# Four instruction orders of an attention stage rearranged: projections later, one evacuation on VectorE, weight splits earlier

## The chip, the cores and the metric

The kernel runs on one core of a Trainium2 chip. A core has a matrix engine (TensorE, PE in the profile, with its weight loads as PEld), a vector engine (VectorE, DVE), a scalar engine (ScalarE, ACT), GpSimd (POOL) and a queue that issues DMAs (SyncE, SP). Each engine works its own instruction list strictly in order and waits at semaphores for the others. The metric is the device time of one execution in microseconds (us), lower is better. The median of three runs before the change is 2721.38 us (2718.41 to 2723.39).

## The reference

Two layers of an encoder trunk are computed for 512 prompt tokens and for 8 running streams of 16 tokens (640 tokens in 5 tiles of 128). Each layer is a half SwiGLU, a mixer, another half SwiGLU and a gated embedding, with layer norms between. The mixer of the second layer is stick-breaking attention over 16 heads of 64; the streams also attend to 1024 cached keys each. What the change touches is this:

```python
def sb_core(q, k, v, q_pos, k_pos):
    z = jnp.einsum('bqhd,bkhd->bhqk', q, k) * SB_SCALE
    mask = k_pos[None, :] < q_pos[:, None]
    log_keep = jnp.where(mask, jax.nn.log_sigmoid(-z), 0.0)
    after = lax.cumsum(log_keep, axis=3, reverse=True) - log_keep
    w = jnp.where(mask, jnp.exp(jax.nn.log_sigmoid(z) + after), 0.0)
    return jnp.einsum('bhqk,bkhd->bqhd', w.astype(v.dtype), v)
```

## The kernel before

The program is a list of stages (`plan_stages`), each written out by hand for every engine. Weights arrive by DMA in units of 512 KB into three slots of `raw`; ACT copies a unit's high part into `ring` (line 970), DVE subtracts to get the low part (line 1285), and every product is made of three matmuls (line 1645). This pair of instructions is called a weight split here.

The attention stage takes the heads as eight pairs, i = 0 to 7. Each pair has ten units of scores (`UNITS`), numbered 0 to 9: units 2, 5, 8 and 9 are the cached samples, the others the prompt. Unit g = 10 i + u passes through a fixed chain:

- PE `scores` writes z to one of four PSUM banks (line 499 helper);
- DVE `neg_abs` (line 1390) writes -|z|, and for samples also max(z, 0) (line 1396);
- ACT `exp_ln` takes Exp and Ln (lines 1032, 1034);
- DVE `softplus` (line 1406) for prompt units, or `sample_sums` (a scan, line 1429, and a subtraction, line 1432) for samples; for samples ACT then does `sample_rows` (Exp, line 1040);
- PE `suffix` (two sums by triangular matrices for prompt units, four transposes at line 605 for samples);
- ACT `weights` (line 1049), PE `values` with the value rows.

Beside the units run the "events" (`STEP_EVENTS`): results that PE writes to just two PSUM banks, 6 and 7, in turn. They are the projections qA, qB, kA, kB of the next pair (A is 384 columns, B is 256), the transposed cached keys kT (su, j) of sample su, each with four transposes (line 531), the transposed own keys kt4 and kt1 (line 522), the totals `tot`, and `past` (line 549), the sample outputs of the pair before. Before PE may write event number k it waits until event k - 2 has been evacuated (`event_bank`). Even kT events, kt4 and all projections are evacuated by ACT (lines 1016, 1018, 1023), odd kT events, kt1, tot and past by DVE (lines 1360, 1362, 1364, 1371). After qB has been evacuated, DVE copies its sample columns into `q_blk` (`sample_queries`, line 1380).

SP issues the cached keys (`load_keys`, line 761) and values (`load_values`, line 771), four DMAs of 256 KB for each sample, and weight units (line 739). Values of a sample wait for `values` of the sample two before, and everything behind them in the queue waits too. In the last pair (i = 7) there is no projection; in its place ACT and DVE split the attention output (`split_o`, lines 1055 and 1438) and the first units of the output weights, and PE begins the output product (`out_early`) as soon as it can.

## Time and profile before

| | us |
|---|---|
| median of three runs | 2721.38 |
| lowest, highest | 2718.41, 2723.39 |
| the profiled execution's own time | 2718.41 |
| its span in the profile | 2716.4 |
| attention stage, first scores of pair 0 to first scores of pair 7 | 1673.74 to 2031.87 |
| first matmul of the output product | 2079.45 |

| engine | busy us | share of the span |
|---|---|---|
| PE | 2591.2 | 95% |
| PEld | 2313.9 | 85% |
| DVE | 1105.0 | 41% |
| ACT | 851.5 | 31% |
| POOL | 78.0 | 3% |

Times in the trace are microseconds from the span's start. A row of a timeline gives the start and the length of a group of like instructions, and in brackets how long the engine sat idle before it and what ended the idleness. Two starts on one engine give the pitch, which is shorter than the lengths printed, since instructions overlap a little in their ends.

### The profile page before, as it was taken

The numbers are of one execution on the slowest core, as the hardware profiler recorded it, in microseconds if no ns is written. First come the engines' busy times: TensorE is split into PE (matmuls) and PEld (weight loads), VectorE is DVE, ScalarE is ACT, GpSimd is POOL, SyncE is SP. The second block draws the span as 40 slices with busy tenths as digits, with TensorE's granted clock in tenths as the row PEclk, the third lists the DMA queues.
The fourth block names the chain that finished last, engine by engine and source line by source line (L and its number), as shares of the span: only waits on it lengthen the run. The fifth ranks groups of instructions, "written<-read, shape, count | busy, mean of one in ns | idle before, by whom it ended". The sixth has DMA issues, their size and how long they took to land. (4 is left out here: it accounts for less than half of the span.)

```text
span 2716.4 us, 37476 instructions
## 1 busy us (share of the span) xinstructions
PE 2591.2 (95%) x16164; PEld 2313.9 (85%) x16164; DVE 1105.0 (41%) x1521; ACT 851.5 (31%) x1271; POOL 78.0 (3%) x169
## 2 busy tenths in 40 slices
PE   7999999989999998899999999999998999999987
PEld 7998998789989987799899877666665899899876
DVE  3322334553232245633233342555555632232365
ACT  3212222232122223522122233555555322132133
POOL 3000000100000000000000001000000000000000
PEclk9999999889999998999999999999999999999999
DMA  5213221322132212232132215666765322232220
GB/s 163 78 59 90 78 69 56 95 80 69 58 94 74 74 59 86 77 92 68 54 105 71 72 60 153 183 177 188 207 181 167 92 86 74 59 94 78 65 90 39
DMA packets 376612, 259.07 MB, mean 95 GB/s; under 512 B 10433, under 2 KB 339137, under 8 KB 376448
## 3 DMA queue, kind: packets, MB, share of 16 engines
q1 hardware_dynamic: 371344, 239.64, 30.3%
q0 software_dynamic: 5104, 17.04, 2.0%
q8 instruction: 128, 2.10, 0.3%
q14 instruction: 36, 0.29, 0.0%
HBM read 248.22 MB, written 8.42 MB: 94 GB/s over the span
## 5 line engine op out<-in xcount | busy, mean ns | idle before, releaser
L1645 PE MATMUL ps<-xt_hi,ring 128*128 128x384 f32 (+1 forms) x6144 | 1353.1, 311 | 37.2 <-DVE xt_lo L1345 15.7
L1645 PEld LDWEIGHTS ps<-xt_hi,ring 128*128 128x128 f32 x6144 | 1042.6, 191 | 53.2 <-issue 20.9
L1645 PE MATMUL ps<-xt_lo,ring 128*128 128x256 f32 (+1 forms) x3072 | 952.5, 310 | 0.0
L1645 PEld LDWEIGHTS ps<-xt_lo,ring 128*128 128x128 f32 x3072 | 586.6, 191 | 0.2
L1645 PE MATMUL ps<-ring,h_hi 128*128 128x512 f32 x1760 | 549.9, 392 | 0.0
L970 ACT ACTIVATE ring<-raw 128x1024 fp32r<-128x1024 f32 x326 | 324.8, 1028 | 442.7 <-PE ps L1645 351.1
L1285 DVE TENSOR_TENSOR ring<-raw,ring 128x1024 fp32r<-128x1024 f32 x326 | 381.7, 1198 | 160.7 <-ACT ring L970 156.5
L1645 PEld LDWEIGHTS ps<-ring,h_hi 128*128 128x128 f32 x1760 | 332.6, 189 | 69.0
L1528 DVE SCALAR_TENSOR_TENSOR act<-act,ps 128x384 f32<-128x384 f32 (+1 forms) x176 | 85.9, 488 | 689.1 <-PE ps L1645 689.1
L1645 PE MATMUL ps<-ring,h_lo 128*128 128x512 f32 x880 | 344.2, 391 | 0.0
L1183 ACT ACTIVATE h_hi<-act 128x384 fp32r<-128x384 f32 (+1 forms) x176 | 82.8, 471 | 647.7 <-DVE act L1528 647.7
L1645 PE MATMUL ps<-ring,xt_hi 128*128 128x512 f32 (+1 forms) x720 | 230.3, 394 | 19.5 <-DVE ring L1285 15.6
L1645 PEld LDWEIGHTS ps<-ring,h_lo 128*128 128x128 f32 x880 | 166.4, 189 | 34.0
L1645 PEld LDWEIGHTS ps<-ring,xt_hi 128*128 128x128 f32 x720 | 139.4, 198 | 50.1 <-DVE ring L1285 14.4
L1177 ACT ACTIVATE act<-ps 128x384 f32<-128x384 f32 (+1 forms) x176 | 77.0, 437 | 255.3 <-PE ps L1645 253.4
L1645 PE MATMUL ps<-ring,xt_lo 128*128 128x512 f32 (+1 forms) x360 | 140.4, 390 | 0.0
L1534 DVE TENSOR_TENSOR h_lo<-act,h_hi 128x384 fp32r<-128x384 f32 (+1 forms) x176 | 86.5, 492 | 92.2 <-ACT h_hi L1183 92.2
L1320 DVE SCALAR_TENSOR_TENSOR x<-x,ps 128x512 f32<-128x512 f32 x50 | 34.2, 685 | 185.6 <-PE ps L1645 185.6
L1645 PEld LDWEIGHTS ps<-ring,xt_lo 128*128 128x128 f32 x360 | 71.4, 198 | 12.5
L531 PEld LDWEIGHTS ps<-ident,k_raw 128*128 128x128 f32 x512 | 56.1, 141 | 30.2 <-issue 19.4
L531 PE MATMUL ps<-ident,k_raw 128*128 128x128 f32 x512 | 70.8, 277 | 10.9 <-DMA k_raw<-in_cache_k_dram 6.8
L1390 DVE TENSOR_SCALAR e_buf<-ps 128x512 int32<-128x512 int32 (+1 forms) x80 | 51.5, 661 | 65.7 <-PE ps L499 65.5
(128 smaller groups left out, 1527.1 us busy)
## 6 DMA issues: line engine op xcount, KB each, us to landing
raw<-in_ffn_w_dram SPq DMA_DIRECT2D x256, 512.0 KB, 4.3
k_raw<-in_cache_k_dram SPq DMA_DIRECT2D x128, 256.0 KB, 5.2
v_raw<-in_cache_v_dram SPq DMA_DIRECT2D x128, 256.0 KB, 4.1
raw<-in_sb_w_in_dram SPq DMA_DIRECT2D x24, 512.0 KB, 6.2
raw<-in_ple_w_gate_dram SPq DMA_DIRECT2D x16, 512.0 KB, 4.1
g_b<-in_ln_g_dram POOLq DMA_DIRECT2D x8, 512.0 KB, 4.1
b_b<-in_ln_b_dram POOLq DMA_DIRECT2D x8, 512.0 KB, 5.5
raw<-in_ffn_w_dram SPq DMA_DIRECT2D x16, 256.0 KB, 3.5
```

Of the source, the lines that this page charges most:

```text
L531: ins = pe.transpose(ps[:, bank, kb * P:(kb + 1) * P], k_raw[:, sample % 2, j, kb, :], ident[:])
L970: se.activation(ring[:, slot_of(u), 0, 0:cols_in(u)], raw[:, raw_slot(u), 0:cols_in(u)], ACT.Copy).then_inc(w_hi_done, 1)
L1177: se.activation(act[:, PART[p]], ps[:, 2 * ((n - 1) % 2), 0:PART[p].stop - PART[p].start], ACT.Silu).then_inc(act_done, 1)
L1183: se.activation(h_hi[:, i, PART[p]], act[:, PART[p]], ACT.Copy).then_inc(h_hi_done, 1)
L1285: ve.tensor_tensor(ring[:, slot_of(u), 1, 0:n], raw[:, raw_slot(u), 0:n], ring[:, slot_of(u), 0, 0:n].bitcast(F32), ALU.subtract).then_inc ...
L1320: ve.scalar_tensor_tensor(dst, dst, ALPHA, ps[:, n % 4, :], ALU.mult, ALU.add).then_inc(x_upd, 1)
L1390: ve.tensor_scalar(e_buf[:, g % 2, 0:n].bitcast(I32), ps[:, g % 4, 0:n].bitcast(I32), SIGN, None, ALU.bitwise_or).then_inc(na_done, 1)
L1528: ve.scalar_tensor_tensor(act[:, PART[p]], act[:, PART[p]], 0.5, ps[:, 2 * ((n - 1) % 2) + 1, 0:PART[p].stop - PART[p].start], ALU.mult, A ...
L1534: ve.tensor_tensor(h_lo[:, i, PART[p]], act[:, PART[p]], h_hi[:, i, PART[p]].bitcast(F32), ALU.subtract).then_inc(h_lo_done, 1)
L1645: return pe.matmul(out, w, xx, start=first, stop=last, skip_group_check=True)
```

## The change

Only orders change, and one evacuation changes engines. No instruction is dropped; on DVE the evacuation of qB is new, on ACT it is gone.

- PE: `suffix` of unit 9 of the pair before moves ahead of projection qA; qB moves behind `suffix` 2 and `values` 1; `past` moves from before `scores` 5 to behind the transposes of kT (2, 0) and (2, 1); kA moves behind `suffix` 5 and `values` 4.
- ACT: `sample_rows` 9 goes behind `exp_ln` 0, `sample_rows` 2 ahead of kT (1, 2), `sample_rows` 5 behind `exp_ln` 6, and `sample_rows` 8 behind `weights` 7 and `exp_ln` 9. The evacuation of kT (0, 0) of the next pair goes behind these two. The weight split of unit 2i + 4 moves from after `exp_ln` 7 to before `exp_ln` 6, and so on DVE from after `softplus` 7 to before `neg_abs` 6.
- DVE: evacuates qB and builds `q_blk` at the end of step 4; `past` goes behind kT (2, 1).
- Last pair: the split of the first three output units moves ahead of unit 8 on both engines. SP loads them one and a half samples later.

```diff
-    4: [("qB",), ("past",)],
-    5: [("kT", 2, 0), ("kT", 2, 1)],
+    4: [("qB",)],
+    5: [("kT", 2, 0), ("kT", 2, 1), ("past",)],
-ON_ACT = ("qA", "qB", "kA", "kB", "kt4")
+ON_ACT = ("qA", "kA", "kB", "kt4")
...
                     values(i - 1, 7)
+                    suffix(i - 1, 9)
                 if follows:
                     project(i + 1, ("qA",))
-                if i:
-                    suffix(i - 1, 9)
...
+                suffix(i, 2)
+                values(i, 1)
                 if follows:
                     project(i + 1, ("qB",))
-                suffix(i, 2)
-                values(i, 1)
-                if i:
-                    transpose_past(i - 1, ("past",))
 
                 scores(i, 5)
                 suffix(i, 3)
                 turn_keys(i, 2, 0)
+                if i:
+                    transpose_past(i - 1, ("past",))
...
+                suffix(i, 5)
+                values(i, 4)
                 if follows:
                     project(i + 1, ("kA",))
-                suffix(i, 5)
-                values(i, 4)
...
-                if i == PAIRS - 2 and su == 2:
+                if i == PAIRS - 1 and su == 0:
                     for key in load_order[raw_at[first_out]:raw_at[first_out] + RAWS]:
...
                     exp_ln(g + 3)
+                    sample_rows(i, 2)
                     turned(i, 1, 1)
...
                     turned(i, 2, 0)
+                    if i < PAIRS - 2:
+                        cvt_to(first_qk + 2 * i + 5)
...
+                    exp_ln(g + 6)
                     sample_rows(i, 5)
-                    exp_ln(g + 6)
...
+                elif name == "qB":
+                    cols = PART[1]
+                    ve.tensor_scalar(q_t[i % 2][:, cols], src[:, 0:cols.stop - cols.start], SCALE, None,
+                                     ALU.mult).then_inc(aux_free_dve, 1)
+                    if i == 0:
+                        ve.wait_ge(q_blk_zero, 2)
+                    ve.wait_ge(aux_free_dve, count)
+                    for h in range(2):
+                        rows = slice(HEAD_DIM * h, HEAD_DIM * (h + 1))
+                        ve.tensor_copy(q_blk[i % 2][rows, :, h, :],
+                                       q_t[i % 2][rows, SEQ:].rearrange("p (b s) -> p b s", s=DEC_SEQ)
+                                       ).then_inc(q_blk_done, 1)
```

On DVE, in pair 4, the rows from `softplus` 3 and 4 (`sp_p`) to `neg_abs` 6 and 7 (`e_buf`, x2) stood like this before (`v_tok` is past, `ring` would be the weight split, line numbers are each kernel's own):

```order
L1406 SCALAR_TENSOR_TENSOR sp_p<-ps,e_buf 128x384 x2
L1371 TENSOR_TENSOR v_tok<-v_tok,ps 64x128 x2
L1390 TENSOR_SCALAR e_buf<-ps 128x512
L1396 TENSOR_SCALAR relu_s<-ps 128x512
L1360 COPY kc_t<-ps 128x512
L1429 SCALAR_TENSOR_TENSOR s_sum<-e_buf,s_sum,relu_s 128x512
L1432 TENSOR_TENSOR relu_s<-ps,s_sum 128x512
L1380 COPY q_blk<-act 64x8x16 x2
L1390 TENSOR_SCALAR e_buf<-ps 128x512 x2
```

The same stretch of the changed kernel:

```order
L1410 SCALAR_TENSOR_TENSOR sp_p<-ps,e_buf 128x384 x2
L1369 TENSOR_SCALAR act<-ps 128x256
L1376 COPY q_blk<-act 64x8x16 x2
L1394 TENSOR_SCALAR e_buf<-ps 128x512
L1400 TENSOR_SCALAR relu_s<-ps 128x512
L1362 COPY kc_t<-ps 128x512
L1385 TENSOR_TENSOR v_tok<-v_tok,ps 64x128 x2
L1433 SCALAR_TENSOR_TENSOR s_sum<-e_buf,s_sum,relu_s 128x512
L1436 TENSOR_TENSOR relu_s<-ps,s_sum 128x512
L1287 TENSOR_TENSOR ring<-raw,ring 128x1024
L1394 TENSOR_SCALAR e_buf<-ps 128x512 x2
```

The evacuation of qB and `q_blk` stand ahead of `neg_abs` 5 now, past stands ahead of the scan of unit 5, and the weight split ahead of `neg_abs` 6 and 7.

On ACT, at the end of pair 3, from kT (3, 2) of this pair to kt4 of the next (`k_tok`), the rows before (`relu_s` is `sample_rows` 8, `wt` is `weights` 7, the second `kc_t` is kT (0, 0) of the next pair, `e_buf` is `exp_ln` 9):

```order
L1016 ACTIVATE kc_t<-ps 128x512
L1040 ACTIVATE relu_s<-relu_s 128x512
L1049 ACTIVATE wt<-ps 128x512
L1016 ACTIVATE kc_t<-ps 128x512
L1032 ACTIVATE e_buf<-e_buf 128x512
L1034 ACTIVATE e_buf<-e_buf 128x512
L1018 ACTIVATE k_tok<-ps 128x512
```

The same stretch of the changed kernel:

```order
L1015 ACTIVATE kc_t<-ps 128x512
L1048 ACTIVATE wt<-ps 128x512
L1031 ACTIVATE e_buf<-e_buf 128x512
L1033 ACTIVATE e_buf<-e_buf 128x512
L1039 ACTIVATE relu_s<-relu_s 128x512
L1015 ACTIVATE kc_t<-ps 128x512
L1017 ACTIVATE k_tok<-ps 128x512
```

The evacuation of kT (0, 0) stood ahead of the Exp and Ln of unit 9 and stands behind them and `sample_rows` 8 now; PE's transposes of kt4 write the bank that it frees.

On ACT in the last pair, from `exp_ln` 7 to `exp_ln` 8 and kT (3, 0), the rows before (`xt_hi` is `split_o`, `ring` the split of output weights):

```order
L1032 ACTIVATE e_buf<-e_buf 128x512
L1034 ACTIVATE e_buf<-e_buf 128x512
L1055 ACTIVATE xt_hi<-v_tok 128x640 x4
L1049 ACTIVATE wt<-ps 128x512
L1032 ACTIVATE e_buf<-e_buf 128x512
L1034 ACTIVATE e_buf<-e_buf 128x512
L1016 ACTIVATE kc_t<-ps 128x512
```

The same stretch of the changed kernel:

```order
L1031 ACTIVATE e_buf<-e_buf 128x512
L1033 ACTIVATE e_buf<-e_buf 128x512
L1048 ACTIVATE wt<-ps 128x512
L1054 ACTIVATE xt_hi<-v_tok 128x640 x2
L969 ACTIVATE ring<-raw 128x1024 x3
L1031 ACTIVATE e_buf<-e_buf 128x512
L1033 ACTIVATE e_buf<-e_buf 128x512
L1015 ACTIVATE kc_t<-ps 128x512
```

The three splits of output weights (`ring`, x3) stand ahead of `exp_ln` 8 now, and on DVE ahead of `neg_abs` 8. Before, they stood behind `exp_ln` 9, four in a row.

## Rows read from the trace of the kernel before

**Rows 1.** The page's first part: busy time of each engine, share, instructions.

```profile
PE 2591.2 (95%) x16164; PEld 2313.9 (85%) x16164; DVE 1105.0 (41%) x1521; ACT 851.5 (31%) x1271; POOL 78.0 (3%) x169
```

**Rows 2.** Busy time by stretch: pair 3, and the output product's start.

```profile
core 0: us, PE busy (x) PEld busy (x) DVE busy (x) ACT busy (x) POOL busy (x), PEclk, DMA share, GB/s
1825.92:1877.60 51.68, 48.90 (x430) 34.79 (x430) 29.41 (x47) 28.64 (x52) 3.69 (x6) 1.00 0.69 190
2079.40:2084.30 4.90, 4.85 (x12) 3.82 (x13) 2.17 (x2) 0.92 (x1) 0.00 (x0) 0.50 0.73 197
```

**Rows 3.** Timeline of PE through pair 3: start, length, instruction, idle before.

```profile
1825.92 1.15 PE L499 MATMUL ps<-act,k_t 64*128 64x128 f32 x12
...
1830.46 0.41 PE L1645 MATMUL ps<-xt_hi,ring 128*128 128x384 f32 x1 [0.34 <-ACT kc_t L1016]
...
1843.94 0.39 PE L1645 MATMUL ps<-xt_hi,ring 128*128 128x256 f32 x1
...
1847.45 1.09 PE L499 MATMUL ps<-wt,v_tok 128*64 128x128 f32 x12
1848.47 0.44 PE L549 MATMUL ps<-ident,o_past 128*128 128x128 f32 x2
...
1851.93 1.09 PE L531 MATMUL ps<-ident,k_raw 128*128 128x128 f32 x8 [0.76 <-DMA k_raw<-in_cache_k_dram]
1852.95 1.13 PE L499 MATMUL ps<-act,k_t 64*128 64x512 f32 x4
...
1858.86 0.41 PE L1645 MATMUL ps<-xt_hi,ring 128*128 128x384 f32 x1 [1.42 <-ACT kc_t L1016]
...
1864.42 1.06 PE L499 MATMUL ps<-kc_t,q_blk 128*32 128x512 f32 x8
...
1876.91 0.76 PE L522 MATMUL ps<-ident,k_t 128*128 128x128 f32 x5
1877.60 1.15 PE L499 MATMUL ps<-q_t,k_t 64*128 64x128 f32 x12
```

**Rows 4.** Timeline of ACT in pair 3, some of its rows.

```profile
1829.73 0.58 ACT L1016 ACTIVATE kc_t<-ps 128x512 f32<-128x512 f32 x1
...
1844.51 0.63 ACT L1040 ACTIVATE relu_s<-relu_s 128x512 f32<-128x512 f32 x1
...
1852.62 0.60 ACT L1016 ACTIVATE kc_t<-ps 128x512 f32<-128x512 f32 x1 [0.26 <-PE ps L531]
```

**Rows 5.** Timeline of DVE in pair 3.

```profile
1842.84 0.69 DVE L1432 TENSOR_TENSOR relu_s<-ps,s_sum 128x512 f32<-128x512 f32 x1
...
1855.11 0.69 DVE L1432 TENSOR_TENSOR relu_s<-ps,s_sum 128x512 f32<-128x512 f32 x1
...
1856.21 1.29 DVE L1390 TENSOR_SCALAR e_buf<-ps 128x512 int32<-128x512 int32 x2
...
1861.26 1.23 DVE L1285 TENSOR_TENSOR ring<-raw,ring 128x1024 fp32r<-128x1024 f32 x1 [0.26 <-ACT ring L970]
...
1875.01 0.69 DVE L1390 TENSOR_SCALAR e_buf<-ps 128x512 int32<-128x512 int32 x1 [1.84 <-PE ps L499]
```

**Rows 6.** Timeline of SP's queue: the load behind `values` 8, pairs 3 and 7.

```profile
1839.52 2.02 SPq L771 DMA_DIRECT2D v_raw<-in_cache_v_dram  x4
...
2044.36 2.03 SPq L771 DMA_DIRECT2D v_raw<-in_cache_v_dram  x4
```

**Rows 7.** Timelines of PE, DVE and ACT in pair 7.

```profile
2042.19 1.09 PE L531 MATMUL ps<-ident,k_raw 128*128 128x128 f32 x8 [3.05 <-DMA k_raw<-in_cache_k_dram]
...
2054.18 1.09 PE L531 MATMUL ps<-ident,k_raw 128*128 128x128 f32 x8
...
2079.45 0.76 PE L1645 MATMUL ps<-ring,xt_hi 128*128 128x512 f32 x1 [3.67 <-DVE ring L1285]
...
2067.09 0.69 DVE L1390 TENSOR_SCALAR e_buf<-ps 128x512 int32<-128x512 int32 x1
...
2075.92 2.93 ACT L970 ACTIVATE ring<-raw 128x1024 fp32r<-128x1024 f32 x3
```

More of the change, by code:

```diff
@@ L1020, in evacuate_event @@
                 else:
-                    dst = (q_t if name[0] == "q" else k_t)[i % 2]
+                    dst = {"qA": q_t, "kA": k_t, "kB": k_t}[name][i % 2]
                     cols = PART["AB".index(name[1])]
                     se.activation(dst[:, cols], src[:, 0:cols.stop - cols.start], ACT.Copy,
-                                  scale=SCALE if name[0] == "q" else 1.0).then_inc(aux_free_act, 1)
+                                  scale=SCALE if name == "qA" else 1.0).then_inc(aux_free_act, 1)
             def attend_act():
@@ L1082, in attend_act @@
                     last = not follows
+                    exp_ln(g)
                     if i:
                         sample_rows(i - 1, 9)
-                    exp_ln(g)
                     turned(i, 0, 1)
@@ L1090, in attend_act @@
                     if i:
-                        save_prompt(i - 1)
+                        weights(g - 1)
                     if follows:
                         cvt_to(first_qk + 2 * i + 4)
+                    if follows:
                         evacuate_event((i + 1, ("qA",)))
                     if i:
-                        weights(g - 1)
+                        save_prompt(i - 1)
                     exp_ln(g + 2)
@@ L1106, in attend_act @@
                         save_samples(i - 1)
-                    sample_rows(i, 2)
                     exp_ln(g + 4)
+                    weights(g + 2)
                     if follows:
                         evacuate_event((i + 1, ("qB",)))
-                    weights(g + 2)
                     exp_ln(g + 5)
@@ L1119, in attend_act @@
                         split_o(1)
+                    exp_ln(g + 6)
                     sample_rows(i, 5)
-                    exp_ln(g + 6)
                     turned(i, 2, 1)
                     weights(g + 4)
+                    if last:
+                        split_o(2)
+                        split_o(3)
                     exp_ln(g + 7)
-                    if last:
-                        for c in range(2, 6):
-                            split_o(c)
-                    if i < PAIRS - 2:
-                        cvt_to(first_qk + 2 * i + 5)
+                    weights(g + 5)
                     if follows:
                         evacuate_event((i + 1, ("kA",)))
-                    weights(g + 5)
+                    if last:
+                        split_o(4)
+                        split_o(5)
+                        cvt_to(first_out + 3)
                     exp_ln(g + 8)
@@ L1140, in attend_act @@
                         evacuate_event((i + 1, ("kB",)))
+                    if last:
+                        split_o(6)
                     turned(i, 3, 1)
+                    weights(g + 7)
+                    exp_ln(g + 9)
                     sample_rows(i, 8)
-                    weights(g + 7)
                     if follows:
                         turned(i + 1, 0, 0)
-                    exp_ln(g + 9)
-                    if last:
-                        split_o(6)
-                        cvt_to(first_out + 3)
-                    if follows:
                         evacuate_event((i + 1, ("kt4",)))
@@ L1371, in evacuate_event @@
                         ve.tensor_tensor(dst, dst, past, ALU.add).then_inc(ot_dve if h == 0 else aux_free_dve, 1)
-            def sample_queries(i):
-                if i == 0:
-                    ve.wait_ge(q_blk_zero, 2)
-                ve.wait_ge(*evacuated((i, ("qB",))))
-                for h in range(2):
-                    rows = slice(HEAD_DIM * h, HEAD_DIM * (h + 1))
-                    ve.tensor_copy(q_blk[i % 2][rows, :, h, :], q_t[i % 2][rows, SEQ:].rearrange("p (b s) -> p b s", s=DEC_SEQ)
-                                   ).then_inc(q_blk_done, 1)
             def attend_dve():
@@ L1443, in turned @@
                     evacuate_event((i, ("kT", su, 2 * half + 1)))
-                sample_queries(0)
+                evacuate_event((0, ("qB",)))
                 turned(0, 0, 0)
@@ L1469, in attend_dve @@
                     softplus(i, 4)
+                    if follows:
+                        evacuate_event((i + 1, ("qB",)))
+                    neg_abs(g + 5)
+                    turned(i, 2, 0)
                     if i:
                         evacuate_event((i - 1, ("past",)))
-                    neg_abs(g + 5)
-                    turned(i, 2, 0)
                     sample_sums(i, 5)
-                    if follows:
-                        sample_queries(i + 1)
+                    if i < PAIRS - 2:
+                        cvt_to(first_qk + 2 * i + 5)
                     if last:
@@ L1486, in attend_dve @@
                     softplus(i, 7)
-                    if i < PAIRS - 2:
-                        cvt_to(first_qk + 2 * i + 5)
                     if last:
@@ L1491, in attend_dve @@
                             split_o(c)
+                        cvt_to(first_out + 3)
                     neg_abs(g + 8)
@@ L1495, in attend_dve @@
                     sample_sums(i, 8)
+                    if last:
+                        split_o(6)
                     turned(i, 3, 1)
@@ L1503, in attend_dve @@
                         evacuate_event((i + 1, ("kt1",)))
-                    if last:
-                        split_o(6)
-                        cvt_to(first_out + 3)
                 cvt_to(first_out + 4)
```

## The prediction

> **What bounds the kernel now.** I read the page's busy times first, then the attention stage pair by pair in the view of stretches, then the timelines of PE, ACT and DVE side by side through one pair, and last the DMA queue. PE is busy for 95% of the span [rows 1], so time can only be won where PE waits, and every new wait of PE is paid in full. The change touches the attention stage alone. Pair 3 stands for pairs 1 to 5: it lasts 51.68 us at a granted clock of 1.00, and PE is busy in 48.90 of them [rows 2]. DVE (29.41) and ACT (28.64) are a little over half busy, but they are used in short chains: PE hands z to DVE, DVE to ACT, ACT back to DVE or to PE. What decides is how far behind PE each link is, and what stands ahead of it in its engine's list.
>
> PE's idle time in pair 3 is in three places [rows 3]: 0.34 us ahead of qA and 1.42 us ahead of kA, both for ACT's evacuation of a kT event two earlier, and 0.76 us ahead of the transposes of kT (2, 0), for a DMA of cached keys. The change shortens or removes the first two: more PE work goes ahead of each projection. But this work needs results that so far had the time of a whole projection to become ready, and ACT and DVE orders change with it. So I follow pair 3 through the new order, in its own times. An evacuation's end on ACT releases PE 0.15 us later: 1829.73 + 0.58 = 1830.31 [rows 4] against 1830.46 [rows 3]. DVE hands to ACT within 0.05. A 512-wide ACT instruction delays the next by about 0.5 (an estimate from lengths of 0.58 to 0.63 that overlap).
>
> **Part 1, `suffix` 9 ahead of qA: 0.** The transposes need `sample_rows` 9, which now stands behind `exp_ln` 0 and ahead of kT (0, 2). The evacuation of kT (0, 2) moves from 1829.73 to about 1830.2, so PE starts `suffix` 9 near 1830.5 and qA near 1831.0 in place of 1830.46. It has done `suffix` 9 (0.53 at pitch) by then. The two cancel.
>
> **Part 2, qB behind `suffix` 2 and `values` 1: +0.9 up to `scores` 5.** PE is through with the earlier work at 1843.94, where qB starts now [rows 3]. `suffix` 2 needs DVE's subtraction, 1842.84 + 0.69 = 1843.53 [rows 5], then `sample_rows` 2, 0.63 long [rows 4], so 1844.2, and PE at 1844.3: a wait of 0.4. `values` 1 needs `weights` 1, which stands behind `sample_rows` 2 and kT (1, 2) on ACT: 1844.2 + 0.4 + 0.6, so 1845.2, PE at 1845.35, another 0.5. Before, qB's 2.98 us (1843.94 to 1846.92) covered both. qB then ends at 1849.35, where `scores` 5 would have stood at 1848.47 without past [rows 3]. DVE's evacuation of qB, with the copies into `q_blk`, stands ahead of `neg_abs` 5; no row has it, its nearest are the 512-wide ones of 0.69. DVE has from 1849.5 to 1850.5, when `scores` 5 is through. I take 0, with 0 and 0.5 as the ends.
>
> **Part 3, the DMA wait hides most of part 2, and past brings it back: +1.0 at `scores` 6.** The keys land a fixed time after `values` 8 frees the queue: issued from 1839.52 [rows 6], used at 1851.93 [rows 3]. This doesn't move, so the 0.9 shrinks the wait of 0.76 to about 0.25 and PE begins kT (2, 0) at 1851.95. Right behind kT (2, 0) and (2, 1) comes past now, and its bank is the one of kT (2, 0). ACT evacuates that from 1852.62 to 1853.22 before [rows 4]; with `scores` 5 later, `exp_ln` 5 and `weights` 3 push it to about 1852.85, so past can start at 1853.6, while PE is free at 1852.95. It ends 0.36 later, 1853.95, against `scores` 6 at 1852.95 before [rows 3].
>
> **Part 4, kA behind `suffix` 5 and `values` 4: +1.9 at `scores` 8.** `suffix` 5 needs `sample_rows` 5, which stands behind `exp_ln` 6, and that needs `neg_abs` 6. On DVE past, the scan, the subtraction and now the weight split stand ahead of it. Past's transposes reach DVE at about 1854.1; two adds 0.6, the scan 1.3, the subtraction 0.7 give 1856.7 (before: 1855.11 + 0.69 = 1855.80 [rows 5]), the split 1.1 to 1.23 gives 1857.85, so `neg_abs` 6 starts there in place of 1856.21 [rows 5]. Its end, 1858.5, then Exp and Ln (1.3) and `sample_rows` 5 (0.6) give 1860.4; PE gets there at 1853.95 + 4.49 = 1858.45, where 4.49 is the work between 1852.95 and 1858.86 less the 1.42 idle. So it waits 2.1, does `suffix` 5 (0.5), waits 0.3 for `weights` 4, does `values` 4 (0.8) and kA (4.24), and reaches `scores` 8 at 1866.3 against 1864.42 [rows 3]: +1.9. The old waits of 0.34 and 1.42 are gone within this number. If no split stood there the wait would be 1.0; that is the low end.
>
> **Part 5, kT (0, 0) of the next pair behind `exp_ln` 9 and `sample_rows` 8: +1.3.** PE writes kt4 into the bank of kT (0, 0), at 1876.91 before, with no wait [rows 3]. Now ACT needs `neg_abs` 9 first, 1875.01 + 0.69 = 1875.70 [rows 5], then Exp and Ln to 1877.05, `sample_rows` 8, and the evacuation, which ends at 1878.05; PE at 1878.2. That is 1.3, and the next pair's `scores` 0 waits behind it.
>
> Pairs 1 to 5: 1.9 + 1.3 = 3.2 each, 16.0. Pair 0 has no DMA wait to eat part of the 0.9, hence 3.2 + 0.8 = 4.0. Pair 6 has no weight split at this place (less 1.1), no DMA wait (plus 0.8), and its part 5 vanishes in the 3.05 us that PE waits for keys at 2042.19 in pair 7 [rows 7] (less 1.3): 1.6.
>
> **Part 6, the last pair: +10.5.** The three output units of 512 KB are now issued between the values behind 2044.36 [rows 6] and the keys for 2054.18 [rows 7]. 2.5 MB took 12.4 us in pair 3 (1839.52 to 1851.93) with latency; at 190 GB/s mean and idle stretches in it [rows 2] the flowing rate is near 290 (an estimate), so 1.5 MB more is 5.4 us: keys at 2060.0, +5.8 (bounds: 3.5 where the rest has slack, 8.3 at the mean rate). `neg_abs` 8, at 2067.09 before [rows 7], gets that delay, and past's bank wait and `exp_ln` 6 as in parts 3 and 4 (+1.3 with the split left out), and behind `split_o` the three new splits on DVE, 3 x 1.2 = 3.6, fed by ACT's 2.93 [rows 7], +4.9 with their waits for each other: together +12. From `neg_abs` 8 to `values` 7 the chain is as before plus `sample_rows` 8 behind `exp_ln` 9 and `split_o` 6 (+1.7), but the splits need not come behind it any more: their 3.67 us of PE wait at 2079.45 [rows 7] go. So the output product starts at +10. It also needs the fourth unit, whose load stands behind the last values, and may wait a microsecond. I take 10.5, bounds 2 and 15.
>
> The sum is 16.0 + 4.0 + 1.6 + 10.5 = 32.1 us, on the profiled execution's own 2718.4: 2750.5. This lies 3.0 under the median of the runs, so 2753.5 in terms of the median.
>
> PE stands idle for some 8 us in that pair. The start of the output product ran at a granted clock of 0.50 after an idle stretch [rows 2, 7], which is 1.2 GHz. I expect such a stretch in the changed kernel too, so nothing is added for it; it would lie somewhat earlier. The Trainium skill, "TensorE: Matmul & The Clock Gate", Part 1, says that an idle array falls to the lower of two clocks and rises after sustained work. By that rule, with which the trace agrees at this place, longer waits inside the pairs could cost more than their own length; that is the fourth rival.
>
> **The rivals.**
> - *The pairs lose, the last pair does not* (+22.6, 2744): the keys in pair 7 land in time or the slack behind 2062 takes the splits in. For it: DVE and ACT had idle time there before. Against it: `neg_abs` 8 stands strictly behind the splits. The sum is 21.6 plus 1.
> - *Half of the per-pair delay is hidden* (+16.5, 2738): if ACT and DVE hand over quicker than I bound, parts 2 to 4 come to +0.6 in place of 1.9 and part 5 stays. 5 x 1.9 + 2 + 1 + 4.
> - *Faster* (-12, 2709): PE's waits for kT go, 7 x (0.34 + 1.42) = 12.3, and nothing takes their place. It is decided at one place, `suffix` 5: `sample_rows` 5 would have to be done when PE reaches it (1858.86 less 1.42 is 1857.44), but DVE's subtraction alone ended at 1855.80 and `exp_ln` 6 with `sample_rows` is 2.6 long from 1856.21 + 0.69. Even without the split this is at 1858.9. So little speaks for it.
> - *The clock falls in each pair* (+57, 2778): a projection kA of 4.24 at half the clock is 4.2 more, six times 25. Against it: after the 3.05 us at 2042.19 PE's transposes kept their length of 1.09 [rows 7].
>
> **How the numbers follow.** The forecast has 0.62, the last pair without loss 0.15, half hidden 0.10, faster 0.05, the clock 0.04, and 0.04 for about nothing. The range, 2737 to 2765, takes in the forecast with the bounds of part 6 (-8, +5) and of parts 2 to 4 (1 us in each of seven pairs), and the first two rivals. Within 0.2% (5.4 us, about what a measurement can tell) 0.04, faster 0.05, slower 0.91.
>
> **What would show it.** PE in pair 3 of the changed kernel waits before `suffix` 5 for ACT's `relu_s` some 2 us, before past for kT's evacuation 0.6, before kt4 1.3, before `values` 1 0.5, while the waits before qA and kA are gone; pairs last 54.9 us; in the last pair PE has an idle stretch of about 8 us that ends with ACT's kT. The forecast is wrong if pairs last under 53, or if the last pair's `neg_abs` 8 is not delayed by the splits.

## The result, and the profile after

The changed kernel takes 2757.37 us (median of 4 runs, 2755.12 to 2759.64) against 2720.59 (2718.41 to 2723.39) of the kernel before in the same comparison: a ratio of 1.0135, 95% interval 1.0117 to 1.0152. It is slower by 36.8 us. The profiled execution took 2757.95 us, its span is 2756.2. The forecast was 2753.5, its range 2737 to 2765.

First the page: busy time of each engine.

```profile
span 2756.2 us, 37476 instructions
PE 2596.5 (94%) x16164; PEld 2315.2 (84%) x16164; DVE 1108.5 (40%) x1529; ACT 844.1 (31%) x1263; POOL 78.1 (3%) x169
```

The work is what it was [rows 1]: PE is busy 5 us longer, the span is 39.8 us longer. So this is mostly waiting, and the timeline says where. The rows of PE in pair 3 that begin with a wait (start, length, instruction, idle before and what ended it):

```profile
1839.62 0.66 PE L605 MATMUL ps<-ident,relu_s 128*128 128x128 f32 x4 [0.31 <-ACT relu_s L1039]
...
1853.55 0.66 PE L605 MATMUL ps<-ident,relu_s 128*128 128x128 f32 x4 [0.24 <-ACT relu_s L1039]
...
1855.06 1.09 PE L499 MATMUL ps<-wt,v_tok 128*64 128x128 f32 x12 [0.84 <-ACT v_tok L1072]
...
1863.29 0.41 PE L549 MATMUL ps<-ident,o_past 128*128 128x128 f32 x2 [0.95 <-ACT kc_t L1015]
...
1870.01 0.66 PE L605 MATMUL ps<-ident,relu_s 128*128 128x128 f32 x4 [1.89 <-ACT relu_s L1039]
1870.87 0.87 PE L499 MATMUL ps<-wt,v_tok 128*64 128x384 f32 x4 [0.20 <-ACT wt L1048]
...
1891.35 0.74 PE L522 MATMUL ps<-ident,k_t 128*128 128x128 f32 x5 [1.20 <-ACT kc_t L1015]
```

From the top: `suffix` 9, `suffix` 2, `values` 1, past, `suffix` 5, `values` 4, kt4. The three waits of [rows 3] (0.34, 1.42 and the DMA's 0.76, 2.52 us in all) are gone, and seven of 5.63 us stand in their place. By stretch, pair 3, pair 4 and three pieces of the last pair (the columns are those of [rows 2]):

```profile
1835.29:1892.02 56.73, 50.83 (x431) 36.42 (x430) 29.89 (x48) 27.67 (x51) 3.87 (x6) 0.97 0.62 174
1892.02:1947.23 55.21, 49.31 (x431) 34.92 (x430) 29.87 (x48) 27.67 (x51) 3.87 (x6) 1.00 0.63 178
2056.43:2104.00 47.57, 31.28 (x269) 18.79 (x268) 26.62 (x43) 25.34 (x45) 3.68 (x6) 0.86 0.65 192
2104.00:2112.00 8.00, 5.96 (x32) 3.29 (x36) 4.58 (x7) 4.05 (x7) 0.00 (x0) 0.58 0.01 2
2125.10:2130.00 4.90, 4.86 (x41) 3.60 (x41) 0.00 (x0) 0.72 (x2) 1.88 (x4) 0.50 0.48 161
```

From the first scores of a pair to those of the next:

| pair | 0 | 1 | 2 | 3 | 4 | 5 | 6 | sum | last pair, to `past` |
|---|---|---|---|---|---|---|---|---|---|
| before | 48.96 | 52.07 | 51.15 | 51.68 | 51.86 | 51.70 | 50.71 | 358.13 | 67.58 |
| after | 54.41 | 55.17 | 55.15 | 56.73 | 55.21 | 55.16 | 54.04 | 385.87 | 84.72 |

The seven periods lose 27.7 us and the last pair 17.1, together 44.9. The span shows 39.8, because the code ahead of and behind the attention stage, which is the same in both, came out 5 us shorter in this execution. In the profiled executions of all kernels of this study the stage begins anywhere between 1668 and 1676 us and what follows `past` takes 615 to 620. That scatter says nothing of the change, so I compare traces by the length of the stage and kernels by their medians.

The last pair: the rows of PE with a wait, then of DVE and ACT at the splits.

```profile
2065.61 1.09 PE L531 MATMUL ps<-ident,k_raw 128*128 128x128 f32 x8 [1.54 <-DMA k_raw<-in_cache_k_dram]
...
2083.96 1.97 PE L531 MATMUL ps<-ident,k_raw 128*128 128x128 f32 x8 [6.84 <-DMA k_raw<-in_cache_k_dram]
...
2106.03 1.94 PE L531 MATMUL ps<-ident,k_raw 128*128 128x128 f32 x8 [7.61 <-ACT kc_t L1015]
...
2114.60 0.66 PE L605 MATMUL ps<-ident,relu_s 128*128 128x128 f32 x4 [1.78 <-ACT relu_s L1039]
...
2116.19 0.50 PE L1649 MATMUL ps<-ring,xt_hi 128*128 128x512 f32 x1
...
2125.14 0.76 PE L1649 MATMUL ps<-ring,xt_hi 128*128 128x512 f32 x1 [4.57 <-DVE ring L1287]
```

```profile
2097.05 3.02 DVE L1442 TENSOR_TENSOR xt_lo<-v_tok,xt_hi 128x640 fp32r<-128x640 f32 x4
2099.99 3.49 DVE L1287 TENSOR_TENSOR ring<-raw,ring 128x1024 fp32r<-128x1024 f32 x3
2103.40 0.68 DVE L1394 TENSOR_SCALAR e_buf<-ps 128x512 int32<-128x512 int32 x1
...
2122.68 1.06 ACT L969 ACTIVATE ring<-raw 128x1024 fp32r<-128x1024 f32 x1 [8.14 <-DMA raw<-in_sb_w_out_dram]
```

The keys come late (6.84 us at kT (2, 0)). `neg_abs` 8 stands behind the three splits. PE waits 7.61 us ahead of the transposes of kT (3, 2), whose bank is that of kT (3, 0), and the evacuation of kT (3, 0) stands behind `exp_ln` 8 on ACT. The output product begins without a wait, 59.76 us after the pair's first scores in place of 47.58 (2079.45 in [rows 7]), and waits 4.57 us for its fourth unit. SP issued that load only behind the last values:

```profile
2069.84 1.64 SPq L738 DMA_DIRECT2D raw<-in_sb_w_out_dram  x3
...
2092.81 22.08 SPq L770 DMA_DIRECT2D v_raw<-in_cache_v_dram  x8
2114.93 1.87 SPq L738 DMA_DIRECT2D raw<-in_sb_w_out_dram  x3
```

Not all of the last pair's 17.1 us is waiting. PE's waits up to `past` grow from 12.8 to 24.7 us, which is 11.8. Its busy time grows by 5.6 us (60.04 against 54.45) for the same matmuls, at a mean granted clock of 0.84 in place of 0.95.

### The profile page after: what moved, and what is told of

Read it like the earlier page. It is cut to its first block and busy times, and to the rows that moved or that the text cites. A ratio compares the mean times of both kernels' runs of the same rounds, so it can differ in the third digit from the quotient of the medians.

```text
span 2756.2 us, 37476 instructions
## 1 busy us (share of the span) xinstructions
PE 2596.5 (94%) x16164; PEld 2315.2 (84%) x16164; DVE 1108.5 (40%) x1529; ACT 844.1 (31%) x1263; POOL 78.1 (3%) x169
## 5 line engine op out<-in xcount | busy, mean ns | idle before, releaser
L1649 PEld LDWEIGHTS ps<-xt_hi,ring 128*128 128x128 f32 x6144 | 1042.7, 191 | 39.8 <-DVE xt_lo L1347 17.5
L1649 PEld LDWEIGHTS ps<-ring,xt_hi 128*128 128x128 f32 x720 | 138.0, 196 | 52.0 <-DVE ring L1287 14.2
L1031 ACT ACTIVATE e_buf<-e_buf 128x512 f32<-128x512 f32 (+1 forms) x80 | 48.8, 610 | 126.8 <-DVE e_buf L1394 126.8
```

The source lines that it names most:

```text
L1031: se.activation(e, e, ACT.Exp).then_inc(el_done, 1)
L1649: return pe.matmul(out, w, xx, start=first, stop=last, skip_group_check=True)
```

## The experiments

Four kernels put one part of the change back, one puts all four back, two do one part alone, and five kernels, two of them built up from the other three, look for the waits that the change was aimed at. "Stage" is the time from the first mask matmul of pair 0 to `past` in the profiled execution: 424.6 us before, 469.5 after. The expectations name an evacuation by its call, `turned(i, su, half)`, which on ScalarE evacuates kT (su, 2 half). So "kT (2, 1)" of b3_kt21 and c2_all is kT (2, 2), the event two ahead of kA, "kT (0, 1)" of c3_qa is kT (0, 2), the one two ahead of qA, and "the transposes of kT (3, 0)" of b2_splits, where PE waits, are those of kT (3, 2).

| kernel | median us | before, same comparison | ratio, 95% interval | stage |
|---|---|---|---|---|
| a1_kt00 | 2752.38 | 2720.73 | 1.0118 (1.0102 to 1.0135) | 460.8 |
| a2_split | 2748.95 | 2720.73 | 1.0102 (1.0087 to 1.0117) | 460.3 |
| a3_tail | 2748.94 | 2720.73 | 1.0101 (1.0086 to 1.0116) | 454.1 |
| a4_past | 2752.11 | 2720.73 | 1.0117 (1.0100 to 1.0134) | 462.7 |
| d_proj | 2728.32 | 2720.92 | 1.0031 (1.0016 to 1.0045) | 432.9 |
| b1_loads | 2728.90 | 2720.92 | 1.0024 (1.0012 to 1.0037) | 433.8 |
| b2_splits | 2725.62 | 2720.92 | 1.0022 (1.0009 to 1.0034) | 433.2 |
| b3_kt21 | 2711.47 | 2720.92 | 0.9969 (0.9956 to 0.9982) | 417.3 |
| b4_keys | 2716.65 | 2722.68 | 0.9979 (0.9968 to 0.9990) | 422.0 |
| c1_tail | 2714.08 | 2722.68 | 0.9970 (0.9957 to 0.9983) | 420.4 |
| c2_all | 2703.27 | 2722.68 | 0.9934 (0.9920 to 0.9949) | 411.2 |
| c3_qa | 2701.07 | 2722.68 | 0.9923 (0.9910 to 0.9935) | 405.2 |

**kT (0, 0) back ahead of `exp_ln` 9** (a1_kt00, the changed kernel with one part undone)

```diff
                     weights(g + 7)
+                    if follows:
+                        turned(i + 1, 0, 0)
                     exp_ln(g + 9)
                     sample_rows(i, 8)
                     if follows:
-                        turned(i + 1, 0, 0)
                         evacuate_event((i + 1, ("kt4",)))
```

> The changed kernel with one ACT step put back: the evacuation of kT (0, 0) of the next pair stands behind weights 7 and ahead of Exp and Ln of unit 9. Theory (part 5 of the prediction): PE's wait of 1.20 us before kt4 goes in each of the seven pair ends, six of which count in the time (the seventh turns into a longer wait for keys in the last pair, now 1.54 us): about 7 us under the changed kernel, near 2750, with pairs 1 to 5 lasting 53.9 to 54.0 us in place of 55.15. Rival: the wait is caused by something behind it that takes its place (kt4's other inputs, or the next scores 0 waiting for weights), then pairs last 55.1 as before and the time stays at 2757.

Measured: 5.0 us below the changed kernel's median, where the theory had 7. The wait ahead of kt4 is gone in every pair, and a pair at full clock lasts 54.08 to 54.18 us in place of 55.16. Part 5 is that wait: 1.20 us seen, about 1.05 recovered. In this trace three pairs (0, 1 and 3) had a granted clock of 0.97, in the changed kernel's two (0 and 3). The stage is 8.7 us shorter, yet the profiled execution took 2759.04 us, longer than the changed kernel's: what lies ahead of the stage and behind it took 9.8 us more.

**The weight split back behind unit 7** (a2_split)

```diff
                     turned(i, 2, 0)
-                    if i < PAIRS - 2:
-                        cvt_to(first_qk + 2 * i + 5)
 ...
                     exp_ln(g + 7)
+                    if i < PAIRS - 2:
+                        cvt_to(first_qk + 2 * i + 5)
                     weights(g + 5)
```

(and in the same way on DVE, behind `softplus` 7)

> The changed kernel with the weight split of unit 2i + 4 put back to where it stood before on both engines (ACT: behind exp_ln 7; DVE: behind softplus 7). Theory (part 4): the split's 1.13 us on DVE stands fully in the chain that suffix 5 waits for, so PE's wait there falls from 1.89 to about 0.76 us in pairs 0 to 5, as it is in pair 6 which has no split: six times 1.13 is 6.8 us less, near 2750. If the lower clock that followed the 1.9 us wait in pairs 0 and 3 came from that wait, about 3 us more go with it (2747). Rival: the wait is set by past's bank and Exp 6, not by the split; then less than 2 us go.

Measured: 8.4 us below. The wait at `suffix` 5 falls from 1.89 to 0.76 us, by 1.13, which is what the split took on DVE. The pairs come out at 51.70, 54.05, 54.06, 54.07, 54.07, 54.06 and 54.07 us: no pair at 56.7 is left. Here is the pair that had the low clock in the changed kernel:

```profile
1834.77:1888.84 54.07, 49.48 (x430) 34.81 (x430) 29.97 (x48) 27.69 (x51) 3.69 (x6) 1.00 0.64 182
```

**`past` back ahead of `scores` 5** (a4_past)

```diff
-    4: [("qB",)],
-    5: [("kT", 2, 0), ("kT", 2, 1), ("past",)],
+    4: [("qB",), ("past",)],
+    5: [("kT", 2, 0), ("kT", 2, 1)],
```

(and PE's and DVE's lists with it)

> The changed kernel with past put back on PE and DVE: its transposes follow qB directly and stand ahead of scores 5, and DVE adds it ahead of neg_abs 5. Theory (parts 3 and 4): past costs PE 0.94 us of waiting for its bank and puts 0.67 us of waiting and 0.6 us of work ahead of the scan of unit 5 on DVE; moved back it costs only its own 0.36 us of PE. The chain to suffix 5 starts 0.36 later and is 1.3 shorter, so pairs 1 to 6 get 0.9 us shorter each: 5 to 6 us less, near 2752. Rival: qB now evacuated by DVE stands ahead of past there, so scores 5 and neg_abs 5 are held up by as much as is won and the time stays within 2 us of 2757.

Measured: 5.3 us below; pairs of 54.1 in place of 55.16. Of the 0.95 at past and 1.89 at `suffix` 5 this is left in pair 3:

```profile
1862.65 1.13 PE L499 MATMUL ps<-act,k_t 64*128 64x512 f32 x4 [0.71 <-ACT wt L1048]
...
1868.34 0.66 PE L605 MATMUL ps<-ident,relu_s 128*128 128x128 f32 x4 [1.20 <-ACT relu_s L1039]
```

The bank wait is replaced by a wait of 0.71 at `scores` 6 for `weights` 3, and the other 0.7 us come from `suffix` 5, whose chain no longer has past's adds (0.60 us on DVE, and 0.67 of idleness ahead of them) in front of the scan.

**The last pair and its loads back** (a3_tail)

```diff
-                if i == PAIRS - 1 and su == 0:
+                if i == PAIRS - 2 and su == 2:
```

(and the three output splits behind unit 9 on both engines)

> The changed kernel with the last pair put back: the three output units are loaded in pair 6 and split behind exp_ln 9 on both engines. Theory (part 6, with what the trace of the changed kernel shows): the stretch from the last pair's first scores to past takes 84.7 us in place of 67.6, and nearly all of the 17 comes from the late loads (6.84 us wait for keys), the splits ahead of unit 8 (7.61 us wait) and the late fourth unit (4.57 us wait): 14 to 17 us less, 2741 to 2743. Rival: the other order changes in the pair (sample_rows 8 behind exp_ln 9, past behind kT (2, 1)) carry half of it; then 7 to 9 us less, near 2749.

Measured: 8.4 us below by the medians, though the stage is 15.4 shorter in the trace, all of it in the last pair (68.3 us from the mask to `past` in place of 83.6). The seven periods are those of the changed kernel to 0.02 us in their sum. The missing 7 us lie outside the stage (it began 2.3 later, and what follows `past` took 4.6 longer), in code that is the same. By the medians the part is worth 8 (the rival's number), by the stage in the trace 15 (the theory's). The next two kernels do its halves alone.

**The loads alone, on the kernel before** (b1_loads)

```diff
-                if i == PAIRS - 2 and su == 2:
+                if i == PAIRS - 1 and su == 0:
```

> The kernel before, with one edit: SyncE issues the loads of the first three output units (1.5 MB) in the last pair, behind the values of sample 4i, in place of the pair ahead of it. All engine orders are as before. Theory (the loads push the keys back, and the late keys are paid): PE waits some 5 to 7 us ahead of kT (2, 0) in the last pair, the wait for keys at the start of that pair (3.05 in rows 7) shrinks by about 1.5, and from scores 0 of the last pair to past takes 71 to 74 us in place of 67.6; the time comes to 2724 to 2728. Rival (the slack behind kT (2, 0) takes the delay in, since the output product waited for the splits anyway): that stretch takes under 69 us, and the time is 2718 to 2722.

Measured: 8.0 us slower by the medians, 9.2 in the stage. Both are a little over the theory's, and the last pair from its first scores to `past` takes 78.2 us where it had 71 to 74. PE in the last pair:

```profile
2040.55 1.97 PE L531 MATMUL ps<-ident,k_raw 128*128 128x128 f32 x8 [3.18 <-DMA k_raw<-in_cache_k_dram]
...
2060.37 1.97 PE L531 MATMUL ps<-ident,k_raw 128*128 128x128 f32 x8 [5.23 <-DMA k_raw<-in_cache_k_dram]
...
2088.18 0.76 PE L1645 MATMUL ps<-ring,xt_hi 128*128 128x512 f32 x1 [3.67 <-DVE ring L1285]
```

The theory had the place right (5.23 us at kT (2, 0), where [rows 7] has none) and the first wait wrong: it does not shrink by moving the output units away, 3.18 against 3.05. The last pair is 10.6 us longer. Its waits come to 17.8 us in place of 12.8, since what stands behind keeps its length, the 3.67 included. The other half is the clock, at 0.87 over the pair in place of 0.95: PE is busy 5.9 us longer, and both groups of kT took nearly twice as long as in [rows 7].

**The splits alone, on the kernel before** (b2_splits)

```diff
                         for c in range(2, 6):
                             split_o(c)
+                        cvt_to(first_out + 3)
 ...
                         split_o(6)
-                        cvt_to(first_out + 3)
```

(on ACT and on DVE)

> The kernel before, with one edit: the three output units are split ahead of unit 8 on ScalarE and VectorE, in place of behind unit 9. The loads stay in the pair ahead, so the data is there long before. Theory (work put ahead of neg_abs 8 is paid, work behind unit 9 too, and the two nearly cancel): neg_abs 8 starts 4 to 5 us later and PE waits 3 to 4 us longer ahead of the transposes of kT (3, 0) or suffix 8; the 3.67 us ahead of the output product (rows 7) go; from scores 0 to past 67 to 70 us, the time 2720 to 2723. Rival (the delay at unit 8 is the larger part of the 17 us that this stretch lost in the changed kernel): 73 us or more, the time over 2726.

Measured: 4.7 us slower by the medians; from the mask to `past` 76.1 us in place of 66.5. That length is the rival's, the time lies between the two (2725.62). PE at kT (3, 2) in the kernel before:

```profile
2069.74 1.07 PE L531 MATMUL ps<-ident,k_raw 128*128 128x128 f32 x8 [2.99 <-ACT kc_t L1016]
```

and here, with the output product:

```profile
2068.98 1.94 PE L531 MATMUL ps<-ident,k_raw 128*128 128x128 f32 x8 [6.39 <-ACT kc_t L1016]
...
2087.54 0.76 PE L1645 MATMUL ps<-ring,xt_hi 128*128 128x512 f32 x1 [6.84 <-DVE ring L1285]
```

The first wait grows from 2.99 to 6.39. The 3.67 us ahead of the output product do go, as the theory had it, but what it did not see is the second row. The product starts with units that are ready and uses them up by 2080.7. The fourth is issued behind the last values at 2076.90 and split at 2086.16. Moving three splits forward turned a wait of 3.67 for the first unit into one of 6.84 for the fourth.

**The projections with the orders that go with them** (d_proj: the changed kernel with all four parts put back)

```diff
-                if i:
-                    suffix(i - 1, 9)
 ...
+                if follows:
+                    project(i + 1, ("qB",))
 ...
-ON_ACT = ("qA", "qB", "kA", "kB", "kt4")
+ON_ACT = ("qA", "kA", "kB", "kt4")
```

(against the kernel before; `suffix` 9 now stands ahead of qA, and kA moves like qB. The evacuation of qB on DVE, the moves of `sample_rows` on ACT, those of `weights` 2 and 5 and `save_prompt`, and the new places of `split_o` in the last pair are left in too, so this is not the projections' move by itself; the moves of `weights` and `save_prompt` are part of the change, though "The change" does not list them)

> The changed kernel with four of its parts put back as in the kernel before: past ahead of scores 5, the weight split behind unit 7, kT (0, 0) of the next pair ahead of exp_ln 9, and the whole last pair with its loads. What is left is the move of the projections (qA behind suffix 9, qB behind suffix 2 and values 1 with its evacuation on VectorE, kA behind suffix 5 and values 4). Theory (the prediction's walk through one pair): the waits ahead of qA and kA, 1.76 us a pair, go, and about 1.3 us ahead of suffix 5, 0.2 to 0.8 ahead of values 1 and 0.3 ahead of values 4 come in their place: periods of 51.5 to 52.5 us in place of 51.7, and the time 2719 to 2725. Rival (the four parts that were put back one at a time took back only 27 of 37 us in the medians, so the move of the projections holds the other 10): periods of 53 us, the time 2728 to 2732.

Measured: the periods are the theory's (51.9 in each of pairs 1 to 6, 50.49 in pair 0, a sum of 361.9 us against 358.1), the time is the rival's, 7.4 us slower. Of the 8.3 us in the stage 3.8 are in the seven periods. The other 4.5 are in the last pair, which has no projection: what it has of the change here are ACT's and DVE's orders and the place of `suffix` 9. No run separates these. Its granted clock is 0.93 against 0.95. The waits of pair 3:

```profile
1830.83 0.66 PE L605 MATMUL ps<-ident,relu_s 128*128 128x128 f32 x4 [0.28 <-ACT relu_s L1039]
...
1844.76 0.65 PE L605 MATMUL ps<-ident,relu_s 128*128 128x128 f32 x4 [0.24 <-ACT relu_s L1039]
...
1846.26 1.09 PE L499 MATMUL ps<-wt,v_tok 128*64 128x128 f32 x12 [0.85 <-ACT v_tok L1072]
...
1854.51 1.13 PE L499 MATMUL ps<-act,k_t 64*128 64x512 f32 x4 [0.72 <-ACT wt L1048]
...
1859.92 0.87 PE L499 MATMUL ps<-wt,v_tok 128*64 128x384 f32 x4 [0.21 <-ACT wt L1048]
```

That is 2.3 us in place of 2.52: the move removes the waits ahead of the projections, as meant, and pays them back at the units that now come first. The 1.3 us that the theory had at `suffix` 5 did not come. That fits the waits ahead of it (0.85, 0.72), which had already made PE later, but no run tests it.

**The wait ahead of kA, by ScalarE's list: kT (2, 2) ahead of `sample_rows` 5** (b3_kt21, on the kernel before)

```diff
+                    turned(i, 2, 1)
                     sample_rows(i, 5)
                     exp_ln(g + 6)
-                    turned(i, 2, 1)
                     weights(g + 4)
```

> The kernel before, with one edit: on ScalarE the evacuation of kT (2, 1) stands ahead of sample_rows 5 and exp_ln 6 in place of behind them. PE's order is as before. Theory (the wait of 1.42 us ahead of kA is for this evacuation's place in ScalarE's list and nothing else): the wait goes in pairs 0 to 6, up to 7 x 1.42 = 9.9 us, less what the later exp_ln 6 costs at suffix 5 or scores 8; periods of 50.3 to 50.8 us, the time 2711 to 2715. Rival (the wait is passed on to suffix 5 or kB, since sample_rows 5 and exp_ln 6 end 0.5 later): periods of 51.3 to 51.8, the time 2717 to 2721.

Measured: 2711.47 us, ratio 0.9969 (0.9956 to 0.9982), the theory's number. The wait ahead of kA is gone in all pairs and none takes its place; PE's kA begins without idleness and pair 3 lasts 50.47, of which 0.98 is the wait for keys. The seven periods are 9.7 us shorter:

```profile
1824.16:1874.63 50.47, 48.89 (x430) 34.84 (x430) 29.42 (x47) 28.75 (x52) 3.68 (x6) 1.00 0.68 195
```

**The keys ahead of the weight unit** (b4_keys, on the kernel before)

```diff
-                u = 2 * i + (4 if su == 0 else 5)
-                if su in (0, 2) and u < 2 * PAIRS:
+                u = 2 * i + (4 if su == 1 else 5)
+                if su in (1, 2) and u < 2 * PAIRS:
```

> The kernel before, with one edit: SyncE issues the load of weight unit 2i + 4 behind the values of sample 4i + 1 in place of sample 4i, so that the keys of sample 4i + 2 are ahead of it in the queue. Theory (the waits of 0.4 to 1.2 us ahead of kT (2, 0) in pairs 1 to 5 are for these keys behind 1 MB of weights): they go, periods of pairs 1 to 6 come to 50.7 us (that of a pair without the wait), the sum of the seven periods to 354 to 355 in place of 357 to 358, and the time to 2716 to 2718. Rival (the wait moves to the next keys or to the weight split, which now has its data later): periods unchanged or above 51.2, the time 2719 to 2723.

Measured: 2716.65, periods of 50.69 to 50.80 in pairs 1 to 6, their sum with pair 0 353.4: the theory's numbers, the sum a little under them. Pairs 1 to 6 wait for no keys at kT (2, 0) any more; the last pair waits 0.27 us, and it is 2 us longer, so the stage is 2.6 us shorter where the medians differ by 6.0.

**The last pair, rearranged** (c1_tail, on the kernel before)

```diff
+                if i == PAIRS - 1 and su == 2:
+                    load_unit(first_out + RAWS)
 ...
+                    cvt_to(first_qk + 2 * i + 4 if follows else first_out + 2)
 ...
+                    if last:
+                        cvt_to(first_out + 3)
```

(two units are split in the pair's first step, the third ahead of unit 7, where the expectation speaks of three and of the fourth; the load of the fourth stands ahead of the last values, its split where it was)

> The kernel before, with the last pair changed alone: the first three output units, loaded in the pair ahead as before, are split in the first step of the last pair (where PE waits 3 us for keys), the fourth is loaded ahead of the last values and split ahead of unit 7. Theory (a split costs where it stands between two links of the chain, not where its engines wait anyway): the 3.67 us ahead of the output product go, the waits at the two keys stay, scores 0 to past takes 62 to 64 us in place of 66.5 to 67.6, the time 2715 to 2718. Rival (3.6 us of splits on both engines in the first step delay neg_abs 1 and 2, and this comes out at scores 4 or at values 1): 66 us or more, the time 2720 or over.

Measured: 2714.08, 8.6 us faster; from the mask to `past` 63.3 us, from the first scores 64.4. The output product waits neither for its first units nor for its fourth; the wait at kT (3, 2) grows from 2.99 to 3.93. The stage is only 4.2 us shorter, so half of the 8.6 does not show there.

**The three together, and kT (0, 2) ahead of `exp_ln` 0** (c2_all, c3_qa)

```diff
                     if i:
                         sample_rows(i - 1, 9)
-                    exp_ln(g)
                     turned(i, 0, 1)
+                    exp_ln(g)
```

(c3_qa; c2_all is without this edit)

> The kernel before with three edits together: kT (2, 1) evacuated ahead of sample_rows 5 on ScalarE, the unit load behind the values of sample 4i + 1, and the new placement of the output splits. Theory (their gains add): 9 to 10 from the first, 3 from the second, 4 from the third, so 2702 to 2706, with periods of 49.7 us. Rival (the waits stand in for each other: in the run with the first edit alone some pairs already had no wait for keys): periods of 49.7 to 50.4, the time 2707 to 2710.

> The three edits together and a fourth: on ScalarE kT (0, 1) is evacuated ahead of exp_ln 0. Theory (the wait of 0.34 us ahead of qA, or of the own keys' scores, is for that place too, like the one ahead of kA): it goes in pairs 0 to 6, 2.4 us in all, periods of 49.4 us, 2 to 2.5 us below the run with three edits. Rival (exp_ln 0 half a microsecond later delays neg_abs and weights 0, and a wait for these comes at scores 4 or values 0): no difference, within 1 us.

Measured: 2703.27 and 2701.07, ratios 0.9934 (0.9920 to 0.9949) and 0.9923 (0.9910 to 0.9935). The gains nearly add in the stage: the three edits alone take 7.4, 2.6 and 4.2 us off it, a sum of 14.2, and c2_all takes 13.4. The medians add less well: 9.4, 6.0 and 8.6 are 24.1, and c2_all has 19.4. All seven periods are 49.70 but pair 0's 48.06, then 49.33 to 49.36 with the fourth edit (46.61 in pair 0). Between these two the intervals overlap, so the fourth edit is shown by the periods (3.6 us in seven pairs), not by the times. Pair 0 gains 1.45 of the 3.6, since its wait ahead of qA had been 1.81 us. In c3_qa pair 3 has a single wait left, 0.38 us ahead of `scores` 6:

```profile
1818.96:1868.32 49.36, 48.71 (x431) 34.91 (x430) 29.42 (x47) 28.46 (x52) 3.71 (x6) 1.00 0.71 199
```

This version is the fastest of the study, 21.6 us below the kernel before and so some 58 below the changed one (36.8 + 21.6, from two comparisons).

## Why the prediction was right, step by step

The forecast was right in sign, size and mechanism: the change takes 2.5 us of waits out of a pair and puts 5.6 in. That the time comes within 3.9 us of it is in part luck: in the trace the stage grew by 44.9 us where the sum had 32.1, and the medians differ by 36.8 only. The terms against the trace:

| step | foreseen | measured |
|---|---|---|
| part 1, `suffix` 9 and qA | 0 | wait of 0.31 in place of 0.34 |
| part 2, `suffix` 2 | 0.4 | 0.24 |
| part 2, `values` 1 | 0.5, for `weights` 1 | 0.84, for `save_samples` |
| part 3, past's bank wait | 0.65 | 0.95 |
| part 4, `suffix` 5, of it the split | 2.1, 1.1 to 1.23 | 1.89, 1.13 (a2_split) |
| part 4, `values` 4 | 0.3 | 0.20 |
| part 5, kt4 | 1.3 | 1.20 |
| pairs 1 to 5, each | +3.2 | +3.5 where the clock held |
| pairs 0 to 6 | +21.6 | +27.7 |
| last pair | +10.5 | +17.1 |

- **Parts 1, 4 and 5** held to 0.3 us, and the experiments that undo the split and kT (0, 0) recovered the length of each.
- **Part 2** missed what stands in ACT's list between `weights` 1 and `exp_ln` 4: `save_samples` of the pair before (0.39 and 0.29 us), which reads the PSUM bank that these value matmuls write; PE waits for it by `past_saved`. The two waits came to 1.1 in place of 0.9. The evacuation of qB cost nothing, as taken: 0.42 and 0.47 us on DVE from 1859.23, with `neg_abs` 5 at 1860.26.
- **Part 3**: the DMA wait was not shrunk to 0.25 but is gone, and the bank wait was 0.95. a4_past shows that the part was worth 1.05 us a pair.
- **Pairs 0 and 6**: pair 6 was foreseen at +1.6 and has +3.3. The kt4 wait stands there as in the others; what the key wait in pair 7 gives back for it (3.05 to 1.54) is booked in pair 7. Pair 0 has +5.4 against +4.0, of which 1.6 is the clock (below). The 3.9 that are left agree with the 4.0 by luck: pair 0 has no `past`, so the 0.65 of part 3 can't be there, and it waits 1.25 us at `suffix` 2, where the later pairs wait 0.24.
- **The fourth rival, the clock**, had a chance of 0.04 for all pairs. It happened in two of them: pairs 0 and 3 ran at 0.97. PE at the start of kA in pair 3, with its matmuls in twos at 0.84 us in place of 0.51:

```profile
1871.67 0.54 PE L1649 MATMUL ps<-xt_hi,ring 128*128 128x384 f32 x1
...
1872.33 0.84 PE L1649 MATMUL ps<-xt_hi,ring 128*128 128x384 f32 x2
...
1875.77 0.51 PE L1649 MATMUL ps<-xt_hi,ring 128*128 128x384 f32 x2
```

  The level is 1.2 GHz for some 3.5 us, and it cost 1.5 us (56.73 against 55.21 in the next pair, with the same waits). The rival's price, 4.2 us for the whole of kA at that level, was too high. Of the 6.1 us by which the pairs were undersized this is 3; five pairs at 0.3 more are 1.5, and pair 6 is the rest.
- **Part 6 is the term that was mis-sized.** Its steps held as far as unit 8: the keys came 5.2 us late against the pair's start (5.8 foreseen) and `neg_abs` 8 11.75 late (12 foreseen; 2103.40 - 2056.43 = 46.97 against 35.22 from [rows 7]). Two things were left out. "Nothing is added" for the low clock was wrong: kT (2, 0) took 1.97 us behind the 6.84 us wait where it had taken 1.09 [rows 7], kT (3, 2) and what follows ran at 0.58 about the 7.61 us wait (the stretch from 2104.00 above), and the product came at +12.2 in place of +10. Over the whole last pair PE's added busy time, 5.6 us, goes with the lower clock. And the fourth unit, "a microsecond", cost 4.57. b2_splits shows this alone: the earlier the first three are ready, the longer PE waits for the fourth, whose load stands behind the last values in SP's queue.

The parts nearly add. The four undone one at a time shorten the stage by 8.7, 9.2, 15.4 and 6.8 us, together 40.0, and d_proj, with all four undone, is 8.3 above the kernel before: 48.3 for 44.9. In the medians it is 27.1 and 7.4, 34.5 for 36.8. What stays open is why a3_tail gave 15 us in its trace and 8 in its median, and in the same way b4_keys 2.6 and 6.0, c1_tail 4.2 and 8.6. One profile can't tell scatter outside the stage from an effect on it.

## What to carry to other kernels

A wait of PE ahead of a large matmul group is removed where its releaser stands too late in its own engine's list. Here one line moved on ScalarE took 9.4 us off. Moving the matmul groups behind other work, with the orders that go with it, won nothing: the seven periods got 3.8 us longer (d_proj), because that work had used the groups' time to become ready. When a move is weighed, walk the list of every engine between the releaser and the instruction that is now first, saves and adds included, and then the queue that issues loads, up to the last unit that the consumer will need and not just the first. Work without a near consumer, like a weight split, belongs where its engines wait anyway: behind unit 7 no wait of PE in the pairs ends at it, ahead of `neg_abs` 6 it cost its full 1.13 us in each of pairs 0 to 5.

## What was unexpected of the hardware

TensorE's granted clock fell after waits of 1.5 to 1.9 us, and not each time. Pairs 1 to 5 of the changed kernel have the same wait (1.89 to 1.90 ahead of `suffix` 5), yet kA ran partly at 1.2 GHz in pair 3 alone and at 2.4 GHz in the others. In a3_tail, whose pairs have the same order, it was pair 3 again, in a1_kt00 pairs 1 and 3: 4 of 15 pairs in three traces. Pair 0 is steadier. In all four kernels that wait 1.54 to 1.55 us there at `suffix` 5 (the changed one, a1_kt00, a3_tail, a4_past) the clock fell behind it, while the wait of 1.81 us ahead of qA earlier in the same pair, which 13 of the 14 traces have, was never followed by the lower level. Nor was 1.42 ahead of kA in the kernel before. The length decides as little in the last pair, at kT (1, 0): after 3.05 us it kept 1.09 us [rows 7], after 3.19 in c1_tail and 3.57 in c3_qa too, but after 2.88 in d_proj and 3.18 in b1_loads it took 1.97. The Trainium skill, "TensorE: Matmul & The Clock Gate", Part 1, ties the clock to how busy the array has been recently. The traces agree in that every low stretch in the attention stage has a wait of PE in it or shortly ahead of it, but show that the length of one wait does not decide it. What does, no run here shows. For a prediction this is a cost with a chance: about 1.5 us each time, in two of the changed kernel's seven pairs, for waits of 1.5 to 1.9 us ahead of kA.
